# Two-block transformer on one core: 512-column matmuls for the upper weight tiles of the second feed-forward part, and more pairs of shifted matmuls

## The reference, cut to what matters

```python
def conv_ffn(h, w_up, conv_w, conv_b, w_down):          # h: 256 x 2048
    L = h.shape[1]
    u = h @ w_up                                        # 2048 x 11264
    up = jnp.pad(u, ((0, 0), (CONV_W // 2, CONV_W // 2), (0, 0)))
    u = sum(up[:, j:j + L] * conv_w[j] for j in range(CONV_W)) + conv_b   # 3 taps along the tokens
    gate, val = jnp.split(u, 2, axis=-1)                # 5632 columns each
    return (jax.nn.silu(gate) * val) @ w_down           # 5632 x 2048

x = x + gt2 * conv_ffn(h2, w_up[l], conv_w[l], conv_b[l], w_down[l])
return rmsnorm(x, g_final)
```

## Time and profile before

| | us |
|---|---|
| three runs | 2955.57, 2983.57, 2980.31 |
| median | 2980.31 |
| the profiled execution, its own time | 2952.37 |
| its span on the core | 2950.3 |
| mean granted TensorE clock | 0.984 |

### The profile page before, as it was taken

The page is one execution under the profiler, slowest core; times in us unless marked ns, Lnnn a source line. Parts: engine busy times, 40 slices in busy tenths (PEclk is TensorE's granted clock), DMA queues, the critical chain, the costliest instruction groups (busy, mean ns, idle before and its releaser), DMA issues.

```text
span 2950.3 us, 55162 instructions
## 1 busy us (share of the span) xinstructions
PE 2832.0 (96%) x23814; PEld 2781.7 (94%) x23814; DVE 2087.0 (71%) x2902; ACT 1347.2 (46%) x1698; POOL 5.1 (0%) x13
## 2 busy tenths in 40 slices
PE   7998888999998999999999999999999999999998
PEld 7998888999998999999999999989699999999998
DVE  6988764698886878787687876545457665665665
ACT  4445423344433554443544545445445544544453
POOL 0000000000000000000000000000000000000000
PEclk9999899999999999999999999999999999999999
DMA  5555201567773687777787775534155655566553
GB/s 203 182 172 169 87 1 65 188 241 273 265 283 130 246 305 283 273 278 284 289 294 270 258 260 193 179 129 150 50 179 172 196 195 185 197 200 193 188 192 122
DMA packets 160450, 591.56 MB, mean 201 GB/s; under 512 B 17840, under 2 KB 17840, under 8 KB 159696
## 3 DMA queue, kind: packets, MB, share of 16 engines
q1 hardware_dynamic: 159264, 579.93, 56.6%
q0 software_dynamic: 944, 8.12, 0.7%
HBM read 585.88 MB, written 2.10 MB: 199 GB/s over the span
## 4 chain that ended last, share of the span: by engine, by line
PE 86%; DVE 9%; ACT 2%; issue 1%; DMA 1%; SPq 0%; DVEq 0%; ACTq 0%
PE bank L465 76%; DVE wlo L1485 3%; PE bank L748 1%; DVE ev L1504 1%; DVE modacc L1718 1%; PE bank L492 1%; PE bank L482 1%; DVE modacc L1471 1%; ACT whi L926 1%; PE bank L643 1%; PE bank L496 1%; PE bank L641 1%; PE bank L635 1%; PE bank L720 1%; PE bank L728 0%
## 5 line engine op out<-in xcount | busy, mean ns | idle before, releaser
L465 PE MATMUL bank<-act,whi 128*128 128x256 f32 x10144 | 1761.2, 279 | 42.9 <-DVE wlo L1485 24.9
L465 PEld LDWEIGHTS bank<-act,whi 128*128 128x128 f32 x10144 | 1546.1, 190 | 48.4 <-DVE wlo L1485 21.8
L1485 DVE TENSOR_TENSOR wlo<-raw,whi 128x1024 fp32r<-128x1024 f32 x906 | 1095.6, 1220 | 459.3 <-ACT whi L926 457.4
L465 PE MATMUL bank<-act,wlo 128*128 128x256 f32 x5072 | 1411.5, 278 | 0.0
L926 ACT ACTIVATE whi<-raw 128x1024 fp32r<-128x1024 f32 x906 | 943.2, 1056 | 801.3 <-PE bank L465 800.5
L465 PEld LDWEIGHTS bank<-act,wlo 128*128 128x128 f32 x5072 | 961.4, 190 | 0.0
L465 PE MATMUL bank<-hid,whi 128*128 128x256 f32 x3456 | 590.3, 276 | 1.3 <-DVE wlo L1485 1.3
L465 PEld LDWEIGHTS bank<-hid,whi 128*128 128x128 f32 x3456 | 520.7, 188 | 1.7 <-DVE wlo L1485 1.1
L465 PE MATMUL bank<-hid,wlo 128*128 128x256 f32 x1728 | 477.6, 276 | 0.0
L1471 DVE SCALAR_TENSOR_TENSOR modacc<-modraw,small,modacc 128x512 f32<-128x512 f32 x480 | 347.8, 745 | 21.4 <-DMA modraw<-mods 15.8
L465 PEld LDWEIGHTS bank<-hid,wlo 128*128 128x128 f32 x1728 | 324.4, 188 | 0.0
(11 more groups left out here) (317 smaller groups left out, 1545.9 us busy)
## 6 DMA issues: line engine op xcount, KB each, us to landing
raw<-stream SPq DMA_DIRECT2D x906, 512.0 KB, 4.6
modraw<-mods SPq DMA_DIRECT2D x192, 512.0 KB, 4.5
h<-x_t SPq DMA_DIRECT2D x4, 512.0 KB, 6.1
memV<-mem_t POOLq DMA_DIRECT2D x1, 2048.0 KB, 9.2
tmp<-ctx_t POOLq DMA_DIRECT2D x1, 2048.0 KB, 9.8
out_t<-tmp SPq DMA_DIRECT2D x4, 512.0 KB, 2.6
cz<-catt POOLq DMA_DIRECT2D x1, 1216.0 KB, 13.3
bias<-na_bias POOLq DMA_DIRECT2D x1, 1024.0 KB, 5.1
```

The costliest lines, as they stand in the source:

```text
L465: mm = pe.matmul(b[:, hf * T:(hf + 1) * T], lhs, rhs, start=(kc == 0 and hf == 0 and n == 0), stop=(kc == ph.chunks - 1 and n == 2), skip_ ...
L1485: ve.tensor_tensor(wlo[:, at % SPL_N, :], raw[:, at % RAW_N, :], whi[:, at % SPL_N, :].bitcast(F32), ALU.subtract).then_inc(split_done, 1)
```

## The change

In the phases `up_r` and `down_r` (now `wide`) one matmul with 512 moving columns takes `whi` against both activation parts. Its output is a whole PSUM bank: columns 0 to 255 for the upper activations, 256 to 511 for the lower ones. The `wlo` matmul adds onto the left half. A block now has a pair of banks, 0 and 1 or 4 and 5. The evacuation first adds the halves: ScalarE copies the right halves of both banks to `scaled`, VectorE adds them to the left halves into `total` (in `stat`). The steps that used to read PSUM read `total`. The new operations are issued by `early`, ahead of the split of slot e+3; the old evacuation stays behind it. `block_free` is still signalled by the last multiply-add.

The pair of shifted matmuls becomes a function of its own. It is called where it was, and also after the slots listed in `SHIFT_AT`: fifteen places in eleven phases ahead of the second feed-forward part, nine inside it. A place is (body, slot).

```diff
-        out += [Phase(f"up_{r}", n, DC, per_body=2 if n % 2 == 0 else 1)]
-        out += [Phase(f"down_{r}", 8, n, per_body=2 if n == 16 else 8)]
+        out += [Phase(f"up_{r}", n, DC, per_body=2 if n % 2 == 0 else 1, wide=True)]
+        out += [Phase(f"down_{r}", 8, n, per_body=2 if n == 16 else 8, wide=True)]
...
-        bank = [es.enter_context(nc.psum_tensor(f"bank{i}", [P, 512], F32)) for i in range(8)]
+        pair0, bank2, bank3 = psum("bank01", [P, 2, 512]), psum("bank2", [P, 512]), psum("bank3", [P, 512])
+        pair1, bank6, bank7 = psum("bank45", [P, 2, 512]), psum("bank6", [P, 512]), psum("bank7", [P, 512])
+        pair = (pair0, pair1)
+        bank = [pair0[:, 0, :], pair0[:, 1, :], bank2, bank3, pair1[:, 0, :], pair1[:, 1, :], bank6, bank7]
...
+        total = stat[:, 0, :].rearrange("p (a b) -> p a b", a=2)
...
                 for j in range(ph.S):
+                    for k, t in enumerate(ends if early else ()):
+                        if t == j:
+                            early(i * ph.K + k, (ph.block0 + k) % 2, k)
+                        elif t - ph.S == j and not first:
+                            early((i - 1) * ph.K + k, (ph.block0 + k) % 2, k)
                     if j >= done:
                         slot_fn(i, j)
...
-                        b = bank[(ph.block0 + k) % 2]
+                        b = pair[(ph.block0 + k) % 2] if ph.wide else bank[(ph.block0 + k) % 2]
...
+                                for hf in range(TT if ph.wide else 0):
+                                    at = slice(ci * NCOL + hf * P, ci * NCOL + (hf + 1) * P)
+                                    pe.matmul(b[:, hf, :].rearrange("p (a t) -> p a t", a=2), whi[:, buf, at], src[:, :, c0 + kc, :],
+                                              start=(kc == 0), stop=False, skip_group_check=True)
+                                    mm = pe.matmul(b[:, hf, 0:T], wlo[:, buf, at], src[:, 0, c0 + kc, :],
+                                                   start=False, stop=(kc == ph.chunks - 1), skip_group_check=True)
...
+                            if (i, j) in SHIFT_AT.get(ph.name, ()):
+                                shifted_columns(src, 6 if ph.name == "naq" else 7)
...
+            SHIFT_AT = {"glu": ((1, 0),), "wout": ((1, 4), (2, 3)), "memk": ((0, 4),), "wo": ((0, 1),),
+                        "w1_0": ((0, 4), (0, 11)), "w2_0": ((1, 0), (1, 9)), "ckv_c": ((0, 3),), "nak_c": ((0, 3),),
+                        "nak_x": ((0, 3),), "naq": ((0, 0), (0, 4)), "wout2": ((0, 0),), "up_0": ((0, 6), (1, 0), (4, 0)), "down_0": ((0, 4),), "up_1": ((0, 1), (4, 0)), "down_1": ((0, 4),), "up_2": ((0, 1),), "down_2": ((0, 4),)}
...
+            def right_half(ph):                     # ScalarE
+                def f(n, b, k):
+                    done(ph, n)
+                    c.at(summed, n)
+                    sc.activation(scaled[:, :, :], pair[b][:, :, T:2 * T], ACT.Copy).then_inc(right_out, 1)
...
                     def f(n, b, k):                 # ScalarE, gated
-                        done(ph, n)
+                        c.at(summed, n + 1)
                         c.at(ev_v, n * EV_UP + EV0)
...
-                            ins = sc.activation(ev[:, 0, hf * T:(hf + 1) * T], b2(b)[:, hf, :], ACT.Identity,
+                            ins = sc.activation(ev[:, 0, hf * T:(hf + 1) * T], total[:, hf, :], ACT.Identity,
...
+            def halves(ph):                         # VectorE
+                def f(n, b, k):
+                    c.at(right_out, n + 1)
+                    ve.tensor_tensor(total, pair[b][:, :, 0:T], scaled[:, :, :], ALU.add).then_inc(summed, 1)
```

More of the change, by code:

```diff
@@ L306, in build, with over @@
         block = es.enter_context(nc.Block())
-        def over(ph, slot_of, evac_fn, extra=None, tail=None):
+        def over(ph, slot_of, evac_fn, extra=None, tail=None, early=None):
             ends = [(k + 1) * ph.slots_per_block - 1 + LAG for k in range(ph.K)]
@@ L334, in over @@
             for j in range(LAG):
+                for k, t in enumerate(ends if early else ()):
+                    if t - ph.S == j:
+                        early((ph.iters - 1) * ph.K + k, (ph.block0 + k) % 2, k)
                 if after and j < min(PRE, after.S):
@@ L456, in body @@
                                 kc = sl * ph.per_slot + ci
-                                for hf in range(ph.ncol // P if not ph.flip else TT):
+                                for hf in range(TT if ph.wide else 0):
[4 more added lines that the diff above has]
+                                                   start=False, stop=(kc == ph.chunks - 1), skip_group_check=True)
+                                for hf in range(0 if ph.wide else ph.ncol // P if not ph.flip else TT):
                                     for n, (wx, ax) in enumerate(((whi, 0), (whi, 1), (wlo, 0))):
@@ L484, in mod_matmuls, with shifted_columns @@
                 mm.then_inc(mod_out, 1)
-                src = hid if ph.name.startswith("w2") else act
+                shifted_columns(hid if ph.name.startswith("w2") else act)
+            def shifted_columns(src, out=7):
                 flat = src[:, 0, :, :].rearrange("p c t -> p (c t)")
                 for n in range(2):
-                    pe.matmul(bank[7][:, 0:T], src[:, 0, DC - 1, n * P:(n + 1) * P], flat[:, 14 * T + P // 4:15 * T + P // 4], start=True, stop=True, skip_group_check=True)
+                    pe.matmul(bank[out][:, 0:T], src[:, 0, DC - 1, n * P:(n + 1) * P], flat[:, 14 * T + P // 4:15 * T + P // 4], start=True, stop=True, skip_group_check=True)
+            SHIFT_AT = {"glu": ((1, 0),), "wout": ((1, 4), (2, 3)), "memk": ((0, 4),), "wo": ((0, 1),),
+                        "w1_0": ((0, 4), (0, 11)), "w2_0": ((1, 0), (1, 9)), "ckv_c": ((0, 3),), "nak_c": ((0, 3),),
+                        "nak_x": ((0, 3),), "naq": ((0, 0), (0, 4)), "wout2": ((0, 0),), "up_0": ((0, 6), (1, 0), (4, 0)), "down_0": ((0, 4),), "up_1": ((0, 1), (4, 0)), "down_1": ((0, 4),), "up_2": ((0, 1),), "down_2": ((0, 4),)}
             def row_sums(out, src, tok, start, stop):
@@ L1007, in phase @@
             def phase(name, evac, extra=None, tail=None):
-                over(PH[name], slot, evac(PH[name]), extra, tail)
+                over(PH[name], slot, evac(PH[name]), extra, tail, early=right_half(PH[name]) if PH[name].wide else None)
+            def right_half(ph):
[3 more added lines that the diff above has]
+                    sc.activation(scaled[:, :, :], pair[b][:, :, T:2 * T], ACT.Copy).then_inc(right_out, 1)
+                return f
             def upper_after(name):
@@ L1427, in _ @@
                 c.end(ev_v, n * EV_UP)
+                c.end(summed, n)
                 first += n
                 phase(f"down_{r}", squared if r == len(FF2_ROUNDS) - 1 else nothing)
+                c.end(summed, PH[f"down_{r}"].nblocks)
             norm(None, split=False)
@@ L1541, in onto @@
                         else:
+                            if ph.wide:
+                                c.at(summed, n + 1)
                             for hf in range(2):
                                 o = h[:, ds(n * 2 + hf, 1), :]
[L1544 removed]
+                                ins = ve.scalar_tensor_tensor(o, total[:, hf:hf + 1, :] if ph.wide else b2(b)[:, hf:hf + 1, :], modt[:, ds(n * 2 + (gate + hf), 1)], o,
                                                               ALU.mult, ALU.add)
@@ L1564, in f @@
                                 o = ev[:, 0, hf * T + do.start:hf * T + do.stop]
-                                ins = ve.scalar_tensor_tensor(o, b2(b)[:, hf, so], par("ff_conv", n * 6 + (6 * first + 3 * hf + j)), o,
+                                ins = ve.scalar_tensor_tensor(o, total[:, hf, so], par("ff_conv", n * 6 + (6 * first + 3 * hf + j)), o,
                                                               ALU.mult, ALU.add)
@@ L1583, in phase @@
                 ph = PH[name]
-                over(ph, slot, evac(ph), extra, tail)
+                over(ph, slot, evac(ph), extra, tail, early=halves(ph) if ph.wide else None)
+            def halves(ph):
+                def f(n, b, k):
+                    c.at(right_out, n + 1)
+                    ve.tensor_tensor(total, pair[b][:, :, 0:T], scaled[:, :, :], ALU.add).then_inc(summed, 1)
+                return f
             def lower_after(q):
@@ L2197, in _ @@
                 c.end(ev_a, 2 * n)
+                c.end(summed, n)
+                c.end(right_out, n)
                 first += n
@@ L2202, in _ @@
                     phase(f"down_{r}", resid(80))
+                c.end(summed, PH[f"down_{r}"].nblocks)
+                c.end(right_out, PH[f"down_{r}"].nblocks)
             norm(h, g("g_final"), into=tmp)
```

7 lines of the change are left out of this document (5 added, 2 removed).

## The result

| | before | after |
|---|---|---|
| median of 16 runs, us | 2955.34 (2950.31 to 2984.91) | 2988.73 (2983.29 to 2991.34) |
| profiled execution, us | 2952.37 | 2989.79 |
| its span, us | 2950.3 | 2988.0 |

The change makes the kernel slower, ratio 1.0094 (95% interval 1.0070 to 1.0118), 37.4 us between the two profiled executions. I had forecast 2936. The time before, too, is not what the first three runs showed: of sixteen runs thirteen lie between 2950 and 2962 and three between 2980 and 2985.

What follows compares the result with a forecast made beforehand. TensorE, busy 96%, was taken as the bound, with only matmul spacing counting in the second feed-forward part. 2952.4 - 22.6 + 8.0 - 6.2 + 1.3 + 1.3 = 2934.2, with run offset 2936 us; range 2926 to 2956.

Steps and rivals of the forecast that it cites:

- Part 1, 512 columns: Second feed-forward part: 512 plus 256 columns replace three 256-column matmuls, triple 329.3 ns for 340.0, 2112 times: -22.6 us.
- the spacing is that of weight loads: TensorE's 256-column stream: weight loads, not columns, set the 113.3 ns; a 512-column matmul would take 216 ns.
- Part 2, the pairs: 24 new pairs cost 0.33 us each, +8.0 us; ending eight slow stretches in earlier phases returns -6.2 us.
- Behind all 22 the spacing is quick: Old pairs in phases with moving activations: quick spacing (113.3 ns) follows each, so new pairs should bring it too.
- Part 3, the evacuation: Blocks of the second part: longer evacuation ends e+4's subtraction at +7.66, wanted at +7.90; 0.24 us to spare, no stall.
- rival D: Evacuation in the second part: 0.24 us cover too thin, TensorE stalls in each of 44 blocks, 2945 to 2962; chance 0.18.
- the one at `down_2`: From `up_2` to `down_2`: third slot needs the last of `hid`, ready at +6.52, wanted at +5.27; +1.3 us, once.
- The tail: Kernel's end: copy and add come between the last matmul and the last block's residual, 0.60 + 0.68; +1.3 us.
- The reference point: Sum made against the profiled 2952.4; two of three runs inferred slow in the second part, 28.3 us dearer.
- B: Second part: pairs don't hold quick spacing behind 512-column matmuls; one slow load per triple, 9.5 us, 2946; chance 0.15.
- C: Second part: columns, not loads, set the spacing; 512 columns cost 226.7 ns, nothing won, 2959; chance 0.12.
- E: Second part: late conversion stalls TensorE per block and drops it to slow spacing at each restart; slower than before; chance 0.05.

Runs made afterwards that it cites:

- e4: Changed kernel without the new pairs and without the lower-weights matmul in the second feed-forward part, so only 512-column matmuls follow one another there; 2846.9 us.
- e1: Kernel before with only the 24 new pairs of shifted matmuls, 256-column matmuls everywhere; 2958.1 us, ratio 0.9981.
- e14: Kernel before with eight new pairs, each behind one plain-fp32 one-column matmul; 2984.2 us, ratio 1.0088.
- e15: Kernel before with one new place only, `up_0` (1, 0): eight one-column matmuls and the pair; median 2958.6 us, ratio 0.9971.
- e5: Changed kernel with eight one-column matmuls ahead of each of the 24 new pairs; 3026.6 us, one run.
- e13: Kernel before with eight one-column matmuls at each of the 24 places and no new pair there; 3028.7 us, one run.

## Why the prediction was wrong, by its steps

**Part 1, 512 columns: wrong, and it decides.** The step "the spacing is that of weight loads" failed. I had two facts: 113.3 lies near the 112 ns of one-column matmuls, and plain-fp32 records with 256 columns run at 216. Both are true and neither was about the new matmul, which takes 235.0 ns where I had 216. `e4` shows that a stream with half the loads isn't faster: 233.3 ns against 226.7. The upper bound that I wrote down, a 512-column matmul as dear as two of 256, was the truth (235.0 for 2 x 117.8), and I excluded a loss because I looked at the quick level only. From the same rows the sum could have read: columns at 113.3 or 117.8 ns per 256, whichever level the stream takes. At the slow one the triple is 3 x 117.8 = 353.4, 28.3 us over 2112 triples; measured 353.3. That the new stream would take the slow level, no row of before could tell.

**Part 2, the pairs: wrong in what they do, near in price.** They cost 0.25 us in place of 0.33. "Behind all 22 the spacing is quick" was right and the inference false: each of the 22 stood behind eight or sixteen records of one-column matmuls, and the new ones don't. Also, 19 of the 22 had a quick stream ahead of them already; only three (641, 959 and 1058 us) turned a slow one. In the profile after, six slow places stayed slow (`wout` 2,3, `memk`, `w2_0` 1,0, `ckv_c`, `nak_x`, `naq` 0,4) and two turned quick (`wout` 1,4 and `wo`); in `e1` none of seven did. What distinguished these two is open. Ahead of the part I had 15 x 0.33 - 6.2 = -1.2 us; the two profiles differ by +4.3 there.

**Part 3, the evacuation: right.** Timeline of VectorE and ScalarE after, one block of `up_1`:

```profile
2562.04 0.60 ACT L1047 ACTIVATE scaled<-bank 128x512 f32<-128x512 f32 x1 [3.49 <-PE bank L478]
2562.53 1.05 ACT L958 ACTIVATE whi<-raw 128x1024 fp32r<-128x1024 f32 x1
```

```profile
2562.66 0.69 DVE L1634 TENSOR_TENSOR stat<-bank,scaled 128x512 f32<-128x512 f32 x1 [2.32 <-ACT scaled L1047]
2563.61 1.23 DVE L1527 TENSOR_TENSOR wlo<-raw,whi 128x1024 fp32r<-128x1024 f32 x1 [0.26 <-ACT whi L958]
2564.76 1.79 DVE L1609 SCALAR_TENSOR_TENSOR ev<-stat,pv,ev 128x255 f32<-128x255 f32 x4
2568.16 3.49 DVE L1527 TENSOR_TENSOR wlo<-raw,whi 128x1024 fp32r<-128x1024 f32 x3
```

TensorE, the last matmul of that block:

```profile
2561.72 0.28 PE L478 MATMUL bank<-act,wlo 128*128 128x256 f32 x1
```

The copy starts 0.32 us behind it. The subtraction for slot e+4 ends at 2568.16 + 1.22 = 2569.38: +7.66, as forecast to the hundredth. TensorE wants it at 24 x 0.3533 = +8.48, so the slower matmuls leave 0.8 us instead of 0.24. From 2225 us on it never waits for L1527 in the part, and rival D fell. All waits of TensorE from 2225 us to the part's end, after:

```profile
PE bank L476 <- DVE hid L1622: 0.7, 1, 0.7
```

That is the one at `down_2`, 0.7 for a forecast 1.3: `hid` is ready at +6.52 and wanted after 16 triples, now at +5.65.

**The tail: right, and more.** From the last matmul to the last sum of squares it is 3.46 us (2970.57 to 2974.03), before 2.02 (2935.09 to 2937.11): +1.4 for a forecast 1.3. Another 0.8 was not in the sum: eight one-column records behind the gap took 1.87 us in place of 1.10, at a lower granted clock (last section). After, then before:

```profile
2974.77 1.87 PE L524 MATMUL bank<-ones,stat 128*128 128x1 f32 x8 [3.92 <-DVE stat L1660]
```

```profile
2937.86 1.10 PE L492 MATMUL bank<-ones,stat 128*128 128x1 f32 x8 [2.50 <-DVE stat L1609]
```

**The reference point: right in kind, wrong in weight.** That the 28 us between runs are the spacing of the second part is supported by `e14` and `e15`, though not proven. But I took it that the pairs would turn a usual 2980 into 2950 and built a chance of 0.71 for "faster" on it. Three runs, two of them slow, are a poor estimate of how often: it is 18 of 71, the median is near 2955, and there was little to rescue.

**The rivals.** The time is what B (0.15, the stream stays slow) and C (0.12, columns set the spacing) give together, and I had them one at a time: C gave 2959 at quick columns, B 2946 with dear ones only once per triple. Together they are 2112 x 13.3 = 28.2 us over before. E (0.05) names times like the measured one, but by stalls and restarts once per block, and there are none. With the measured 4.3 ahead of the part, 1.9, 0.7 and 2.2 that is 2952.4 + 37.3 = 2989.7; the profiled execution took 2989.8. Only the 28.2 follows from the spacing; the other terms are read off the two profiles.

## What to carry to other kernels

Merging two matmuls with the same weights wins only if the weight load sets their spacing; before pricing it, check the distance against the columns as well, and ask for one row in which the number of loads differs and the columns don't. When a trace shows one stream at two spacings, price a change at both, and don't assume that a changed mix of instructions lands on the better one. When a device seems to end a bad state every time, count how often that state was there at all, and list what else stands beside the device every time, before it is moved elsewhere alone.

## What the hardware showed that I had not expected

- The fp32r streams here have a price per moving column that changes with where the activations lie in SBUF: 113.3 to 120 ns per 256 columns at a granted clock of 1.00, with the same instructions. 64 bytes (skew 112 to 128) take the kernel with 512 columns in the second part from 2983.6 to 3044.2 us, one run each.
- At the place of this kernel (skew 112) there are two spacings, 113.3 and 117.8, that last for hundreds of microseconds and can be set: eight one-column matmuls lead to slow (24 of 24), these and the pair to quick (24 of 24). What keeps the state isn't known from these runs; that moving reads meet weight reads is a guess that no run tests.
- Behind the closing gap of TensorE the granted clock was 0.50 after, its lower level of 1.2 GHz, and 0.91 on the mean before. Windows behind the gap, after and before (all engines):

```profile
2974.80:2976.60 1.80, 1.80 (x8) 1.75 (x8) 0.00 (x0) 0.42 (x1) 0.00 (x0) 0.50 0.00 0
```

```profile
2937.90:2938.90 1.00, 1.00 (x8) 0.98 (x8) 0.00 (x0) 0.41 (x1) 0.00 (x0) 0.91 0.00 0
```

The change made that gap longer, 3.9 us for 2.5, but its length isn't what decided. In `e5` the same eight records behind a gap of 3.92 took 1.05 us, and in `e13` behind one of 2.50 they took 1.87:

```profile
3012.37 1.05 PE L527 MATMUL bank<-ones,stat 128*128 128x1 f32 x8 [3.92 <-DVE stat L1663]
```

```profile
3013.55 1.87 PE L503 MATMUL bank<-ones,stat 128*128 128x1 f32 x8 [2.50 <-DVE stat L1620]
```

So the 0.8 us of the tail belong to the profiled execution, not surely to the change.
